# Expert weight rows to partitions in runs of eight (down: four), one contiguous 16 KB piece per partition

## The chip, the cores and the metric

The kernel runs on one core of a Trainium2 chip. The metric is the device time of one execution in microseconds (us); smaller is better. Three runs of the kernel before took 1603.82, 1595.23 and 1598.3 us, so the median is 1598.3 us.

## The reference

A two-layer backbone over 256 latent tokens and 256 context tokens of width 1024. Each layer has an attention mixer and then a mixture of experts. Cut to the part that matters here:

```python
def moe_ffn(h, w_router, b_router, w_gate, w_up, w_down):
    s = sigmoid(h @ w_router)                     # (N, 16)
    # one group of four experts, then the best two experts inside it
    out = 0
    for e in range(16):
        y = (silu(h @ w_gate[e]) * (h @ w_up[e])) @ w_down[e]   # 1024 -> 512 -> 1024
        out = out + combine[:, e:e + 1] * y
    return out
```

Layer 0 sends all 512 tokens through it, layer 1 only the 256 latent tokens. All weights are float32. The sum over the 1024 features (and over the 512 hidden units) may be taken in any order, as long as both operands of a product use the same one.

## The kernel before, in words

**Stages.** Twelve chunks of the modulation matrix (L529, each 2 MB), a norm and projections of layer 0, attention, the output projection with the second norm (`out_project`), the router and the lists of tokens per expert, then the experts; the same again for layer 1. TensorE, VectorE, ScalarE, GpSimd and SyncE each have their own program, tied together by semaphores that are written out by hand.

**Weights.** SyncE issues every weight load in program order into a ring of six slots of 16 KB per partition (`load`, L363 to L368). A load waits until the chunk that lay in its slot six chunks ago is used up (`chunks_used`). One expert takes three slots, gate, up and down, of 2 MB each, so the ring holds two experts.

**Layout of a chunk.** TensorE contracts over the 128 partitions, so the 1024 rows of gate and up are split in eight blocks of 128. Before, block k holds rows 128k to 128k+127 and partition p has row 128k+p of it: `"e (k p) f -> e p k f"` (L409, L410). In DRAM a partition's data are eight pieces of 2 KB that lie 256 KB apart. For down the 512 rows are four blocks of 128, four pieces of 4 KB per partition (L411).

**One expert** (`pair`, L754 on TensorE, L1281 on VectorE, L1666 on ScalarE). GpSimd gathers the expert's token rows from `h_dram` (L1857). TensorE transposes them in eight blocks (`rows_T`, L749); ScalarE writes the upper part (L1646), VectorE the rest (L1268). Weights are split likewise into an upper part (ScalarE, L1662) and a rest (VectorE, L1277), and 48 matmuls form gate and up (L767 to L769, three for each block and matrix). ScalarE applies silu (L1672), VectorE multiplies by up out of PSUM (L1287), TensorE transposes the product in four blocks (L779), ScalarE copies it (L1676), and 16 float32 matmuls with down follow (L788). The result goes to DRAM from ScalarE's queue (L1690). TensorE's order in one expert is written by hand: the 48 matmuls, the transposes of the next expert's rows, the four transposes of the product, the 16 matmuls of down.

**Before the experts** (`out_project`). For each tile of 128 tokens VectorE adds the attention result to x (L1182, L1187), ScalarE sums the squares (L1626), and VectorE writes the normed and modulated row into `htok` with two operations on 128x1024 (L1171, L1172). From there it is stored to `h_dram` (L1623) and transposed for the router (L677, L685). Layer 0 has four such tiles, layer 1 has two.

**At the start** SyncE issues three modulation chunks, six small broadcast loads (L393), the router's weights (L394), x and ctx (L395, L396) and then the other chunks. All seven small loads count on one semaphore, `wide_loaded`, on which VectorE waits before L1008. Behind L1008 on VectorE stand L1009, L1010 and the copy L1029, which TensorE needs before L520.

Of the kernel before, what the change touches and what calls it, by code (L numbers as in the profile page):

```python
# [22 lines left out]
P = 128  # L23
D = 1024
KD = D // P
SEQ, CTX = 256, 256
NT = (SEQ + CTX) // P
LT = SEQ // P
# [5 lines left out]
SLOTS = 6  # L34
# [78 lines left out]
def build(nc, a, consts_dram, out_dram, dbg=None, cap=P):  # L113
# [5 lines left out]
    ds = bass.ds  # L119
# [58 lines left out]
    with ctx:  # L178
# [56 lines left out]
        def mod(l, s, r):  # L235
# [48 lines left out]
        xg_hi, xg_lo = ([rq_r[:, (2 * j + i) * D:(2 * j + i + 1) * D].rearrange("p (k n) -> p k n", k=KD) for i in range(2)]  # L284
                        for j in range(2))

        def blocks_of(region, o, n):
            return region[:, o:o + n * CH].rearrange("p (k n) -> p k n", k=n)
        quarter = [[blocks_of(rz_r, 2 * D, 4)], [blocks_of(rz_r, 4 * D, 4)],
# [72 lines left out]
        def _(sp):  # L362
# [28 lines left out]
            modulation(M0, 0, 0, 3)  # L391
            for dst, src in wide:
                sp.dma_start(dst, src.partition_broadcast(P)).then_inc(sem("wide_loaded"), 16)  # L393
            sp.dma_start(wr_sb.rearrange("p (k e) -> p k e", k=KD), a["w_router"].rearrange("(k p) e -> p k e", p=P)).then_inc(sem("wide_loaded"), 16)  # L394
            sp.dma_start(xt[:, 0:LT, :], a["x"].rearrange("a (t p) d -> p (a t) d", p=P)).then_inc(sem("x_loaded"), 16)  # L395
            sp.dma_start(xt[:, LT:NT, :], a["ctx"].rearrange("a (t p) d -> p (a t) d", p=P)).then_inc(sem("x_loaded"), 16)  # L396
            modulation(M0 + 3, 0, 3, MODC - 3)
# [8 lines left out]
                load(n, slotk[n % SLOTS], view(a["even_w_out"][0], CH, i * CH))  # L406

            def experts(base, l):
                gate = a["w_gate"][l].rearrange("e (k p) f -> e p k f", p=P)  # L409
                up = a["w_up"][l].rearrange("e (k p) f -> e p k f", p=P)  # L410
                down = a["w_down"][l].rearrange("e (j p) d -> e p j d", p=P)  # L411
                with sp.Fori(0, NE // 2) as it:
                    for u in range(2):
                        e = it * 2 + u
                        for j, w in enumerate((gate, up, down)):
                            n = base + 3 * u + j
                            s = slotk[n % SLOTS] if j < 2 else slot[n % SLOTS].rearrange("p (j n) -> p j n", j=4)
                            load(n, s, w[ds(e, 1)].rearrange("e p k f -> (e p) k f"), it=it)

            def overflow(l):  # L420

                sp.wait_ge(sem(f"flag_set{l}"), at(f"flag_set{l}", 1))
                over = sp.value_load(flag_i[l][0:1, :], min_val=0, max_val=1)
                with sp.If(over > 0):
                    mats = [(a["w_gate"][l], FF), (a["w_up"][l], FF), (a["w_down"][l], D)]

                    sp.wait_ge(sem(f"y_v{l}"), at(f"y_v{l}", NE))
                    with sp.Fori(0, ROUNDS[l]) as r:
                        with sp.Fori(0, NE) as e:
                            for j in range(3):  # L430

                                if j == 0:
                                    sp.wait_ge(sem(f"over_xT{l}"), at(f"over_xT{l}", r * NE + e + 1))
                                else:
                                    sp.wait_ge(sem(f"over_used{l}"), at(f"over_used{l}", (r * NE + e) * 3 + j))
                                sp.dma_start(over_w[j], mats[j][0][ds(e, 1)].rearrange(
                                    "a (k p) n -> p (a k) n", p=P)).then_inc(sem(f"over_loaded{l}"), 16)
                sp.nop()
            modulation(MA, 1, *PARTS[0])
            experts(X0, 0)  # L440
# [530 lines left out]
        def _(ve):  # L971
# [188 lines left out]
            def out_project(l):  # L1160

                g = 0
                T = TL[l]

                def token_rows(t):
                    rms(rstd[:, t:t + 1], 1, t)
                    if t >= 2:

                        ve.wait_ge(sem(f"h_hi{l}"), at(f"h_hi{l}", t - 1))
                        ve.wait_ge(sem(f"h_stored{l}_{t % 2}"), at(f"h_stored{l}_{t % 2}", 16 * (t // 2)))  # L1170
                    link(V.scalar_tensor_tensor(htok[t % 2], xt[:, t, :], rstd[:, t:t + 1], bc[2 + t // LT], ALU.mult, ALU.mult))  # L1171
                    V.tensor_tensor(htok[t % 2], htok[t % 2], bc[4 + t // LT], ALU.add).then_inc(sem(f"h_ready{l}"), 1)  # L1172

                def token_cols(t):
                    ve.wait_ge(sem(f"h_lo{l}"), at(f"h_lo{l}", t + 1))
                    V.tensor_copy(hT[:, 0:4, t * P:(t + 1) * P], bank[4 + 2 * (t % 2)][:, :].rearrange("p (k n) -> p k n", k=4))\
                     .then_inc(sem(f"h_v{l}"), 1)
                for i in range(2):
                    for t in range(T):
                        product_done(ve, f"out_mm{l}", O0 if l == 0 else O1, [T, T], i, t)  # L1180
                        tm = rk[:, (g % 4) * 512:(g % 4 + 1) * 512]
                        ins = V.tensor_tensor(tm, bank[g % 4][:, :], bc[t // LT][:, i * 512:(i + 1) * 512], ALU.mult)  # L1182
                        ins.then_inc(sem(f"out_v{l}"), 1)
                        g += 1
                        ve.wait_ge(sem(f"out_v{l}"), at(f"out_v{l}", g))
                        xs = xt[:, t, i * 512:(i + 1) * 512]
                        V.tensor_tensor(xs, xs, tm, ALU.add).then_inc(sem(f"x_add{l}"), 1)  # L1187
                        if i == 0:
                            r = len(gate_list(l)) + t
                            broadcast(f"bc{l}", bc_list(l), range(r, r + 1))  # L1190
                        if i == 1:
                            if t >= 1:
                                token_cols(t - 1)
                            token_rows(t)
                token_cols(T - 1)

            def experts(l):
# [83 lines left out]
                def pair(it, last_pair):  # L1281
                    for u in range(2):
                        e = it * 2 + u
                        quarter_lo(u, e, 3)
                        ve.wait_ge(sem(f"silu_ready{l}"), at(f"silu_ready{l}", e + 1))
                        ve.wait_ge(chunks_used, e * 3 + (X0 if l == 0 else X1) + 2)
                        V.tensor_tensor(act_[u], sg[u], bank[3][:, :], ALU.mult).then_inc(sem(f"act_ready{l}"), 1)  # L1287
                        if not (last_pair and u == 1):
                            rows_lo(1 - u, e + 1)
                            for q in range(3):  # L1290
                                quarter_lo(1 - u, e + 1, q)
                        ve.wait_ge(sem(f"y_mm{l}"), at(f"y_mm{l}", e + 1))
                        ve.wait_ge(sem(f"y_stored{l}_{u}"), at(f"y_stored{l}_{u}", it * 16))
                        V.tensor_copy(ybuf[u][:, 0:512], bank[5][:, :]).then_inc(sem(f"y_v{l}"), 1)
# [12 lines left out]
                with ve.If(over > 0):  # L1307
                    ve.wait_ge(sem(f"y_stored{l}_0"), at(f"y_stored{l}_0", 8 * NE))
                    with ve.Fori(0, ROUNDS[l] * NE) as i:
# [2 lines left out]
                            V.tensor_copy(xgT[0][:, 4 * h:4 * h + 4, :], bank[h][:, :].rearrange("p (k n) -> p k n", k=4))\  # L1312
                             .then_inc(sem(f"over_xgT{l}"), 1)
                        ve.wait_ge(sem(f"over_silu{l}"), at(f"over_silu{l}", i + 1))
                        V.tensor_tensor(act_[0], sg[0], bank[3][:, :], ALU.mult).then_inc(sem(f"over_act{l}"), 1)
                        ve.wait_ge(sem(f"over_used{l}"), at(f"over_used{l}", i * 3 + 3))
                        for h in range(2):
                            V.tensor_copy(ybuf[0][:, 512 * h:512 * h + 512], bank[5 + h][:, :]).then_inc(sem(f"over_y{l}"), 1)
# [625 lines left out]
```

## Time and profile before

| | |
|---|---|
| median of three runs | 1598.3 us (1595.23 to 1603.82) |
| span of the profiled execution | 1598.7 us |
| TensorE busy | 1408.6 us, 88% of the span |
| VectorE, ScalarE busy | 803.2 us, 572.6 us |
| bytes moved | 327.33 MB, mean 205 GB/s |
| mean granted TensorE clock | 0.936 of full speed |

The span runs from the first to the last instruction of one profiled execution. It is the profiled execution's own time here and lies 0.4 us above the median of the runs. A matmul's row shows its duration, while matmuls follow one another more closely than that; the distance between starts is what an engine really spends. Idle time of an engine that nothing waits for costs nothing.

### The profile page before, as it was taken

The page shows a single profiled execution, that of the slowest core. Times are in us where ns is not written, and L with a number is a line of the kernel's source. Part 1 is how long each engine was busy: PE and PEld are TensorE (multiplying, and loading weights), DVE is VectorE, ACT ScalarE, POOL GpSimd, SP SyncE. Part 2 cuts the span into 40 slices and gives each one's busy share as a digit, 9 for nine tenths or more (in the row PEclk, how much of TensorE's full clock was granted, in tenths as well). Part 3 has the DMA queues.
Part 4 walks back from the last instruction along what each step waited for, and adds up shares of the span by engine and source line. Part 5 has one row for each costly group of instructions (what it writes and reads, how often), then busy time and mean ns, then how long its engine had stood idle before and what let it go on. Part 6 is the DMA issues. An engine that isn't in the chain of part 4 may idle for free.

```text
span 1598.7 us, 16348 instructions
## 1 busy us (share of the span) xinstructions
PE 1408.6 (88%) x6170; PEld 939.9 (59%) x6170; DVE 803.2 (50%) x1040; ACT 572.6 (36%) x830; POOL 115.7 (7%) x106
## 2 busy tenths in 40 slices
PE   6999959898977997999999999887994999999991
PEld 1229844477865544666666652756953666666660
DVE  0115231567865343555555536565835455555553
ACT  2004121235452113555555521513412444444451
POOL 0000032000000003000000004020002000000002
PEclk9999988898978998999999999897996999999996
DMA  9970000100007155999999999360012799999942
GB/s 328 385 249 35 0 0 27 53 1 1 1 1 263 66 190 177 349 363 363 362 361 363 350 335 347 115 237 18 1 53 98 259 364 362 363 363 362 362 172 92
DMA packets 138594, 327.33 MB, mean 205 GB/s; under 512 B 6133, under 2 KB 10538, under 8 KB 138410
## 3 DMA queue, kind: packets, MB, share of 16 engines
q1 hardware_dynamic: 125706, 282.43, 49.5%
q0 software_dynamic: 6784, 23.09, 3.9%
q10 hardware_dynamic: 6048, 21.04, 3.3%
q8 instruction: 37, 0.61, 0.2%
q14 instruction: 19, 0.16, 0.0%
HBM read 305.51 MB, written 21.04 MB: 204 GB/s over the span
## 4 chain that ended last, share of the span: by engine, by line
PE 78%; DVE 8%; ACT 6%; issue 3%; DMA 2%; POOL 1%; SPq 1%; POOLq 0%; DVEq 0%; ACTq 0%
PE bank L788 14%; PE bank L767 7%; PE bank L769 7%; PE bank L768 7%; PE bank L638 5%; PE bank L700 5%; PE bank L529 5%; PE bank L546 3%; PE bank L630 3%; PE bank L620 3%; PE bank L601 3%; PE bank L602 3%; PE bank L603 3%; ACT region_q_r L1646 2%; PE bank L861 1%
## 5 line engine op out<-in xcount | busy, mean ns | idle before, releaser
L1277 DVE TENSOR_TENSOR ring_r<-ring,region_z_r 128x2048 fp32r<-128x2048 f32 (+1 forms) x128 | 253.5, 2022 | 144.8 <-ACT region_z_r L1662 144.8
L788 PE MATMUL bank<-ring,region_h 128*128 128x512 f32 x512 | 228.2, 598 | 23.8 <-ACT region_h L1676 23.8
L1662 ACT ACTIVATE region_z_r<-ring 128x2048 fp32r<-128x2048 f32 (+1 forms) x128 | 210.0, 1691 | 75.7 <-PE bank L769 75.7
L768 PE MATMUL bank<-ring_r,region_q_r 128*128 128x512 f32 x512 | 200.6, 392 | 0.0
L767 PE MATMUL bank<-region_z_r,region_q_r 128*128 128x512 f32 x448 | 188.8, 421 | 2.8 <-DVE region_q_r L1268 2.8
L769 PE MATMUL bank<-region_z_r,region_q_r 128*128 128x512 f32 x448 | 176.0, 393 | 0.0
L788 PEld LDWEIGHTS bank<-ring,region_h 128*128 128x128 f32 x512 | 94.6, 190 | 138.4 <-issue 131.0
L638 PEld LDWEIGHTS bank<-region_z,region_h 128*128 128x128 f32 x832 | 113.9, 198 | 14.9 <-issue 7.1
L1601 ACT ACTIVATE region_h<-bank,small 128x512 f32<-128x512 f32 (+1 forms) x128 | 77.7, 607 | 123.6 <-DVE small L1125 103.6
L638 PE MATMUL bank<-region_z,region_h 128*128 128x64 f32 x832 | 111.0, 273 | 2.5 <-DVE region_h L1133 2.4
L768 PEld LDWEIGHTS bank<-ring_r,region_q_r 128*128 128x128 f32 x512 | 97.2, 190 | 26.6 <-issue 7.2
L767 PEld LDWEIGHTS bank<-region_z_r,region_q_r 128*128 128x128 f32 x448 | 85.1, 190 | 27.5 <-issue 6.7
L1133 DVE COPY region_h<-bank 128x512 f32<-128x512 f32 (+1 forms) x128 | 75.6, 591 | 41.9 <-PE bank L630 40.9
L1646 ACT ACTIVATE region_q_r<-bank 128x512 fp32r<-128x512 f32 x64 | 35.0, 595 | 170.7 <-PE bank L749 170.7
L769 PEld LDWEIGHTS bank<-region_z_r,region_q_r 128*128 128x128 f32 x448 | 84.9, 190 | 18.4
L529 PE MATMUL bank<-ring,small 128*2 128x512 f32 x192 | 90.2, 627 | 5.2 <-DMA ring<-in_w_mod 4.3
L601 PE MATMUL bank<-region_k_r,region_q_r 128*128 128x512 f32 (+3 forms) x256 | 88.8, 347 | 0.6 <-DVE ring_r L1055 0.6
L602 PE MATMUL bank<-ring_r,region_q_r 128*128 128x512 f32 (+3 forms) x256 | 88.3, 345 | 0.0
L603 PE MATMUL bank<-region_k_r,region_h_r 128*128 128x512 f32 (+3 forms) x256 | 88.3, 345 | 0.0
L1287 DVE TENSOR_TENSOR region_h<-region_h,bank 128x512 f32<-128x512 f32 x32 | 22.0, 688 | 126.0 <-PE bank L769 126.0
L546 PE MATMUL bank<-ring,small 128*2 128x512 f32 x192 | 84.3, 592 | 0.8 <-issue 0.5
L700 PE MATMUL bank<-ring,region_q 128*128 128x512 f32 x192 | 84.1, 593 | 0.0
(257 smaller groups left out, 1847.2 us busy)
## 6 DMA issues: line engine op xcount, KB each, us to landing
ring<-in_w_gate SPq DMA_DIRECT2D x32, 2048.0 KB, 9.5
ring<-in_w_up SPq DMA_DIRECT2D x32, 2048.0 KB, 11.0
ring<-in_w_down SPq DMA_DIRECT2D x32, 2048.0 KB, 9.7
ring<-in_w_mod SPq DMA_DIRECT2D x24, 2048.0 KB, 17.2
y_rows<-region_k ACTq DMA_DIRECT2D x32, 512.0 KB, 7.7
ring<-in_even_w_in SPq DMA_DIRECT2D x3, 2048.0 KB, 7.8
ring<-in_even_w_out SPq DMA_DIRECT2D x2, 2048.0 KB, 8.0
ring<-in_odd_w_in SPq DMA_DIRECT2D x2, 2048.0 KB, 13.2
```

Of the source, the lines that this page charges most:

```text
L529: last = mm(bank[j % 2][0:2, :], silu.rearrange("p (r k) -> p k r", r=2)[:, k, :], slotk[(M0 + j) % SLOTS][:, k, :], start=k == 0, stop=k ...
L601: mm(out, hh, wh, start=k == 0, stop=False)
L602: mm(out, hh, wl, start=False, stop=False)
L603: last = mm(out, hl, wh, start=False, stop=k == KD - 1)
L638: last = mm(out, probsT[(b + u - 1) % 2][:, j * P:(j + 1) * P], v, start=j == 0, stop=j == len(vs) - 1)
L700: last = mm(bank[g % 4][:, :], oT[:, k, t * P:(t + 1) * P], slotk[n % SLOTS][:, k, :], start=k == 0, stop=k == KD - 1)
L767: mm(bank[2 + j][:, :], xg_hi[u][:, k, :], wh, start=k == 0, stop=False)
L768: mm(bank[2 + j][:, :], xg_hi[u][:, k, :], wl, start=False, stop=False)
L769: last = mm(bank[2 + j][:, :], xg_lo[u][:, k, :], wh, start=False, stop=k == KD - 1)
L788: last = mm(bank[5 + h][:, :], actT[u][:, j, :], w[:, j, h * 512:(h + 1) * 512], start=j == 0, stop=j == 3)
L1277: ins = V.tensor_tensor(slotk_r[s_][:, k:k + n, :], slotk[s_][:, k:k + n, :], part.bitcast(f32), ALU.subtract)
L1662: ins = A(part, slotk[n % SLOTS][:, k:k + m, :], ACT.Copy)
```

## The change

Partition p now holds rows 8p to 8p+7 of gate and up and rows 4p to 4p+3 of down, which is one contiguous piece of 16 KB in DRAM. Block k of the contraction is then made of the rows 8p+k. The other operand follows: `htok` is written so that its k-th block of 128 columns holds the features 8j+k, by reading x and the two modulation rows with a step of eight elements; the router's weights are loaded in the same order; and the product of silu and up is written so that block k holds the hidden units 4j+k, by reading both inputs with a step of four elements. The writes stay contiguous. Number, order and shape of instructions on each engine stay as they are.

```diff
+        def strided(ap, n):
+            return ap.rearrange("p (j k) -> p k j", k=n)
...
-            sp.dma_start(wr_sb.rearrange("p (k e) -> p k e", k=KD), a["w_router"].rearrange("(k p) e -> p k e", p=P)).then_inc(sem("wide_loaded"), 16)
+            sp.dma_start(wr_sb.rearrange("p (k e) -> p k e", k=KD), a["w_router"].rearrange("(p k) e -> p k e", p=P)).then_inc(sem("wide_loaded"), 16)
...
-                gate = a["w_gate"][l].rearrange("e (k p) f -> e p k f", p=P)
-                up = a["w_up"][l].rearrange("e (k p) f -> e p k f", p=P)
-                down = a["w_down"][l].rearrange("e (j p) d -> e p j d", p=P)
+                gate = a["w_gate"][l].rearrange("e (p k) f -> e p (k f)", p=P)
+                up = a["w_up"][l].rearrange("e (p k) f -> e p (k f)", p=P)
+                down = a["w_down"][l].rearrange("e (p j) d -> e p (j d)", p=P)
...
-                            s = slotk[n % SLOTS] if j < 2 else slot[n % SLOTS].rearrange("p (j n) -> p j n", j=4)
-                            load(n, s, w[ds(e, 1)].rearrange("e p k f -> (e p) k f"), it=it)
+                            load(n, slot[n % SLOTS], w[ds(e, 1)].rearrange("e p f -> (e p) f"), it=it)
...
-                    link(V.scalar_tensor_tensor(htok[t % 2], xt[:, t, :], rstd[:, t:t + 1], bc[2 + t // LT], ALU.mult, ALU.mult))
-                    V.tensor_tensor(htok[t % 2], htok[t % 2], bc[4 + t // LT], ALU.add).then_inc(sem(f"h_ready{l}"), 1)
+                    ht = htok[t % 2].rearrange("p (k j) -> p k j", k=KD)
+                    link(V.scalar_tensor_tensor(ht, strided(xt[:, t, :], KD), rstd[:, t:t + 1], strided(bc[2 + t // LT], KD), ALU.mult, ALU.mult))
+                    V.tensor_tensor(ht, ht, strided(bc[4 + t // LT], KD), ALU.add).then_inc(sem(f"h_ready{l}"), 1)
...
-                        V.tensor_tensor(act_[u], sg[u], bank[3][:, :], ALU.mult).then_inc(sem(f"act_ready{l}"), 1)
+                        V.tensor_tensor(act_[u].rearrange("p (k j) -> p k j", k=4), strided(sg[u], 4), strided(bank[3][:, :], 4), ALU.mult).then_inc(sem(f"act_ready{l}"), 1)
```

The loads and the product of the overflow branch (L436, L1315), which runs only when an expert gets more than 128 tokens, are changed in the same way.

## Rows read from the trace of the kernel before

**Rows 1.** The page: the span of the profiled execution
```profile
span 1598.7 us, 16348 instructions
```

**Rows 2.** A stretch of the experts: PE PEld DVE ACT POOL busy, clock, DMA share, GB/s
```profile
1430.00:1470.00 40.00, 38.48 (x152) 26.26 (x151) 23.27 (x18) 19.95 (x21) 1.89 (x2) 1.00 0.99 363
```

**Rows 3.** Who waited for whom, 680 to 940 us: PE's wait (us, times, longest)
```profile
PE bank L788 <- ACT region_h L1676: 9.8, 13, 0.8
```

**Rows 4.** Instructions in order of time, one expert of layer 1: start, us, engine, line
```profile
1297.81 7.13 PE L788 MATMUL bank<-ring,region_h 128*128 128x512 f32 x16 [0.76 <-ACT region_h L1676]
...
1310.62 0.37 SPq L368 DMA_DIRECT2D ring<-in_w_gate  x1
...
1315.48 1.02 PEld L749 LDWEIGHTS bank<-con,region_k 128*128 128x128 f32 x8
...
1315.90 0.69 DVE L1287 TENSOR_TENSOR region_h<-region_h,bank 128x512 f32<-128x512 f32 x1 [3.92 <-PE bank L769]
1316.34 1.08 ACT L1646 ACTIVATE region_q_r<-bank 128x512 fp32r<-128x512 f32 x2 [5.28 <-PE bank L749]
...
1316.65 0.66 PE L779 MATMUL bank<-con,region_h 128*128 128x128 f32 x4
1317.34 0.60 ACT L1676 ACTIVATE region_h<-bank 128x512 f32<-128x512 f32 x1
...
1318.07 7.13 PE L788 MATMUL bank<-ring,region_h 128*128 128x512 f32 x16 [0.76 <-ACT region_h L1676]
```

**Rows 5.** The page: two DMA queues (weights; stores); then issue of a load to landing
```profile
q1 hardware_dynamic: 125706, 282.43, 49.5%
...
q10 hardware_dynamic: 6048, 21.04, 3.3%
...
ring<-in_w_gate SPq DMA_DIRECT2D x32, 2048.0 KB, 9.5
```

**Rows 6.** Groups of VectorE by line and shape: busy us, mean ns of one
```profile
L1287 DVE TENSOR_TENSOR region_h<-region_h,bank 128x512 f32<-128x512 f32 x32 | 22.0, 688 | 126.0 <-PE bank L769 126.0
...
L1171 DVE SCALAR_TENSOR_TENSOR region_k<-x,small,region_z 128x1024 f32<-128x1024 f32 x6 | 7.7, 1285 | 0.2
L1172 DVE TENSOR_TENSOR region_k<-region_k,region_z 128x1024 f32<-128x1024 f32 x6 | 7.4, 1225 | 0.2
```

**Rows 7.** VectorE multiplies by a per-partition scalar, by line: min/median/max ns
```profile
L1406 DVE TENSOR_SCALAR small<-small x4: 234/235/235, 436.8 to 488.5; 128x8 f32<-128x8 f32 x4
...
L1343 DVE TENSOR_SCALAR region_z<-region_z,small x4: 341/1884/2431, 229.3 to 239.9; 128x256 f32<-128x256 f32 x4
...
L1049 DVE TENSOR_SCALAR region_z<-x,small x8: 752/754/2767, 119.0 to 1002.4; 128x1024 f32<-128x1024 f32 x8
```

**Rows 8.** Instructions in order of time, out_project: two rows of each layer
```profile
551.51 1.23 DVE L1172 TENSOR_TENSOR region_k<-region_k,region_z 128x1024 f32<-128x1024 f32 x1
...
553.60 1.04 PE L677 MATMUL bank<-con,region_k 128*128 128x128 f32 x8
...
1207.88 1.22 DVE L1172 TENSOR_TENSOR region_k<-region_k,region_z 128x1024 f32<-128x1024 f32 x1
...
1209.16 1.97 PE L677 MATMUL bank<-con,region_k 128*128 128x128 f32 x8
```

**Rows 9.** The start: chain; PE's gap; issue to landing of b_router, of L368's second load
```profile
17.35 12.19 DMA small<-in_w_router
...
43.23 6.96 PE bank L529 x16
...
31.19 1.86 PE L520 MATMUL bank<-con,region_k 2*128 2x2 f32 x8 [2.88 <-DVE region_k L1029]
...
small<-in_b_router SPq DMA_DIRECT2D x1, 8.0 KB, 9.1
...
L368 SPq DMA_DIRECT2D ring<-in_w_mod x2: 3604/3996/4389, 22.7 to 26.4; - x2
...
DMA to landing us min/median/max: 19.1/19.1/19.1
```

More of the change, by code:

```diff
@@ L436, in overflow @@
                                 sp.dma_start(over_w[j], mats[j][0][ds(e, 1)].rearrange(
-                                    "a (k p) n -> p (a k) n", p=P)).then_inc(sem(f"over_loaded{l}"), 16)
+                                    "a (p k) n -> p (a k) n", p=P)).then_inc(sem(f"over_loaded{l}"), 16)
                 sp.nop()
@@ L1314, in experts @@
                         ve.wait_ge(sem(f"over_silu{l}"), at(f"over_silu{l}", i + 1))
-                        V.tensor_tensor(act_[0], sg[0], bank[3][:, :], ALU.mult).then_inc(sem(f"over_act{l}"), 1)
+                        V.tensor_tensor(act_[0].rearrange("p (k j) -> p k j", k=4), strided(sg[0], 4), strided(bank[3][:, :], 4), ALU.mult).then_inc(sem(f"over_act{l}"), 1)
                         ve.wait_ge(sem(f"over_used{l}"), at(f"over_used{l}", i * 3 + 3))
```

## The prediction

> **What bounds the kernel now.** I began with the span, 1598.7 us [rows 1], 0.4 us above the median of the runs shown; every sum below is made against it. Next I took the busy time by stretch, because the change promises faster weight loads and these matter only where something waits for them. During the experts the DMA engines look full: a share of 0.99 at 363 GB/s, while TensorE is busy 38.48 of 40 us at a granted clock of 1.00 [rows 2]. Both could be the bound, so the list of waits decides. From 680 to 940 us, thirteen experts, TensorE waits for ScalarE's copy L1676 (13 times 0.75 us) and for no DMA [rows 3]. The timeline says the same. Two L788 groups start 1318.07 - 1297.81 = 20.26 us apart. The load of a gate chunk issued at 1310.62 lands 9.5 us later, at 1320.1, and its slot is first read while the next expert's down product runs, from 1318.07 + 20.26 = 1338.3 [rows 4, 5]. It is ready about 18 us early. So the experts are bound by TensorE and by the short chain that it waits for, and the DMA engines are busy because they are asked for just that much: 3 x 2 MB of weights plus two transfers of 0.5 MB, 7.34 MB in 20.26 us, are 362 GB/s.
>
> The chain is what the reader should see in rows 4. TensorE loads its last row transposes (L749) until 1316.50. The four transposes of the product (L779) start only at 1316.65, right after VectorE's product L1287 has ended at 1315.90 + 0.69 = 1316.59. They end at 1317.31, ScalarE's copy L1676 starts at 1317.34, and L788 after it. L1287 thus has no slack at all: each ns that it grows is a ns per expert.
>
> **The change part by part.**
>
> *Weight loads.* The same 96 loads of 2 MB, now 128 pieces of 16 KB each. Nothing waits for them, so their gain is costed at nothing; the cover is the 18 us above. Are large pieces slower? The weight queue moved 282.43 MB in 125706 packets with 49.5% of 16 engines' span: 0.495 x 16 x 1598.7 / 125706 = 101 ns for a mean of 2247 B, 22.3 B/ns. The queue of the stores has mean packets of 3479 B and 0.033 x 16 x 1598.7 / 6048 = 140 ns each, 24.9 B/ns [rows 5]. Larger packets go faster here. I expect a smaller DMA share and no time. SyncE issues as many DMAs at the same points as before; what a load issued earlier or landed earlier would trigger is nothing, since each issue waits for a used chunk.
>
> *Router weights.* A partition's 512 B come as one piece instead of eight of 64 B. This one is on the path: VectorE waits for the load until 17.35 + 12.19 = 29.54, and TensorE stands for 2.88 us until 31.19 [rows 9]. The small load just ahead of it in the queue, b_router, has 128 pieces and takes 9.1 us from issue to landing; the router's has 1024 and takes 12.19 [rows 9]. With 128 pieces it should land at 17.35 + 9.1 = 26.5, and the gap closes: a gain of 2.9 us. It can't be much more, for the fourth modulation chunk is late next. The fifth is issued at 26.4 and lands 19.1 us later, at 45.5; the fourth lies 2 MB ahead of it, 5.8 us at 363 GB/s, so it lands near 39.7, and TensorE now takes it at 43.23 [rows 2, 9]. Bounds 0 (the load stays slow) and 43.2 - 39.7 = 3.5 us.
>
> *Strided reads on VectorE, the main term.* L1287 reads both inputs with a step of 16 B (one of them in PSUM), L1171 and L1172 read with a step of 32 B; writes stay contiguous. No large operation of the trace does this, so the price is bounded. From below: nothing; L1287 takes 688 ns and L1172 1225 ns for twice the elements, 1.05 ns per element, and a read with a step may well keep that rate [rows 6]. From above I use the nearest row, L1406: eight elements, read and written in place with a step of 16 B (heads lie four floats apart), by a per-partition scalar. Its contiguous kin, L1343 with 256 elements at 341 ns at least and L1049 with 1024 at 752 ns, give 0.535 ns per element and a fixed 204 ns, so eight contiguous elements would take 208 ns. L1406 takes 235 [rows 7]. The 27 ns over are up to 3.4 ns per element, 3.9 in all; if I take the fixed part from L1049 alone, at half the 1.05 ns above (220 ns), it is 1.9 ns per element in all. The row is small and its excess may belong to the instruction and not to its elements. I take 2.1 ns, twice the contiguous rate, since L1406 is the nearest row by its step and this lies at the careful end of its 1.9 to 3.9. Then L1287 grows by 512 x 1.04 = 0.53 us and L1171 and L1172 by 1.07 us each.
>
> Where this lands:
> - L1287, 32 experts, no slack: 32 x 0.53 = +17.0 us (bounds 0 and 32 x 1.46 = 47). Behind it on VectorE stand the rests of the rows and weights; VectorE is busy 23.27 of 40 us [rows 2], so they have room.
> - Layer 1, two tiles: L1172 of the second tile ends at 1209.10 and TensorE's L677 follows at 1209.16 [rows 8]. VectorE is the path through both tiles, since L1182 of the second stands right behind L1172 of the first: 2 x 2 x 1.07 = +4.3 us.
> - Layer 0, four tiles: L1172 of the first ends at 552.74, TensorE comes for it at 553.60 behind other products [rows 8]. Of 2.13 us, 0.86 is covered: +1.3 us. The later tiles have more cover as TensorE's products of the output projection take 7 us each; I put +0.1 on them.
>
> Sum: 1598.7 + 17.0 + 4.3 + 1.4 - 2.9 = 1618.5 us, +1.2%.
>
> L1406 spends more than its contiguous kin [rows 7]. The Trainium skill has a rule that would make it so and that speaks against this change: "SBUF — State Buffer", section Door 1: The DMA port swizzle, tells of 16-byte lines that want at least two accesses each for full rate, which a step of four floats never gives. By that rule, with which rows 7 agree as far as they reach, the time lies above 1595.8 us; it names no price.
>
> **The rivals.**
>
> *R1, strided reads cost nothing.* VectorE takes one float32 element per cycle wherever it lies, and L1406's 27 ns are fixed cost. For it: rows 6 have 1.05 ns per element for PSUM and SBUF inputs alike. Against it: rows 7. Time: 1598.7 - 2.9 = 1595.8, no change by the measure. This is the other side of my forecast; it decides at a price of 0.13 ns per element: there the strided terms, 22.7 us at 1.04 ns, are 2.9 us and the start pays for them. The Trainium skill's page "VectorE: DVE Perf Modes", section Mode 1× (REGULAR) — the baseline, would give this time: it says that this mode works with any step, at one result per cycle.
>
> *R2, a steeper price,* near the 3.9 ns bound, say because the PSUM input is worse than SBUF. L1287 +1.46 us, 47 us; L1171 and L1172 +2.9 us each, about 12 us in layer 1 and 7 in layer 0: 1598.7 + 66 - 3 = 1662. Only the upper reading of one small row speaks for it. A price of 3.1 ns, twice my increase, would give about 1642.
>
> *R3, the 16 KB pieces are slow.* Few long pieces per engine could lower the rate. The ring hides it until a layer's 15 further periods have eaten 18 us, so 1.2 us per period, a rate under 7.34 MB / 21.5 us = 342 GB/s. At 300 GB/s a period is 24.5 us and the time 1598.7 + 2 x (15 x 4.2 - 18) = 1689. Rows 5 speak against it.
>
> *R4, the loads are cut into small pieces again,* so the change is not what it says. Then the packets stay as many, and no term of my sum moves, for the loads were costed at nothing.
>
> **How the numbers follow.** A measurement of this kernel tells about 0.5% (8 us) from no change. Twice the rate cost, or near it (1610 to 1626): 0.50. R1: 0.37, times from 1593 to 1599. R2: 0.06. R3: 0.03. A gain over 8 us, from the start and from landings that I do not see: 0.04. R4 changes none. Slower 0.58, same 0.37, faster 0.05 follow (a small price between R1 and mine lies on the border). The range has to take in R1, so 1592 to 1625; the forecast's own range is 1610 to 1626.
>
> **What would show it.** Right: L1287 at about 1.22 us, L1171 and L1172 at about 2.3 us; the distance of L788 groups 20.8 instead of 20.26 us with TensorE idle about 0.7 us before L779; the router's load landing near 26.5 us and L520 starting at about 28.4; the weight queue with some 70000 packets fewer (the experts' 64 x 1024 + 32 x 512 become 96 x 128) and a DMA share below 0.99. Wrong: L1287 still at 0.69 us (R1), far above 1.3 us (R2), a wait of ScalarE's L1662 or TensorE's L788 for a DMA (R3), or 125706 packets again (R4).

## The result, and the profile after

The changed kernel took 1617.9 us (median of four runs, 1614.9 to 1619.8) beside 1598.1 us (1595.2 to 1603.8) for the kernel before: a ratio of 1.0108, 95% interval 1.0081 to 1.0135, so 12.9 to 21.6 us longer. The profiled execution has a span of 1616.0 us. In its lines L1287 has become L1291, L1171 and L1172 have become L1175 and L1176, L749 L752, L779 L782, L788 L791, L677 L680, L520 L523, L529 L532, L546 L549, L1029 L1032; the issues of x (L395) and of the chunks (L368) are L399 and L372.

The page, span and weight queue (packets, MB, share of 16 engines):

```profile
span 1616.0 us, 16348 instructions
...
q1 hardware_dynamic: 55178, 282.43, 47.0%
```

The groups of VectorE by line and shape (busy us, mean ns), the answer to [rows 6]:

```profile
L1291 DVE TENSOR_TENSOR region_h<-region_h,bank 128x512 f32<-128x512 f32 x32 | 34.7, 1083 | 125.9 <-PE bank L772 125.9
...
L1175 DVE SCALAR_TENSOR_TENSOR region_k<-x,small,region_z 128x1024 f32<-128x1024 f32 x6 | 12.5, 2091 | 0.2
L1176 DVE TENSOR_TENSOR region_k<-region_k,region_z 128x1024 f32<-128x1024 f32 x6 | 12.1, 2018 | 0.2
```

The product went from 688 to 1083 ns, 0.395 us or 0.77 ns per element more; the two operations on `htok` grew by 806 and 793 ns for 1024 elements, 0.79 and 0.77 ns per element. A step of 16 B and one of 32 B cost the same for each element.

One expert of layer 1 in order of time (start, us, engine, line, and in brackets how long the engine stood before it and for whom), the answer to [rows 4]:

```profile
1310.37 7.13 PE L791 MATMUL bank<-ring,region_h 128*128 128x512 f32 x16 [0.76 <-ACT region_h L1680]
...
1328.46 1.09 DVE L1291 TENSOR_TENSOR region_h<-region_h,bank 128x512 f32<-128x512 f32 x1 [3.92 <-PE bank L772]
1328.90 1.09 ACT L1650 ACTIVATE region_q_r<-bank 128x512 fp32r<-128x512 f32 x2 [5.28 <-PE bank L752]
1329.61 0.66 PE L782 MATMUL bank<-con,region_h 128*128 128x128 f32 x4 [0.31 <-DVE region_h L1291]
1330.30 0.60 ACT L1680 ACTIVATE region_h<-bank 128x512 f32<-128x512 f32 x1 [0.31 <-PE bank L782]
1331.02 7.13 PE L791 MATMUL bank<-ring,region_h 128*128 128x512 f32 x16 [0.76 <-ACT region_h L1680]
```

The distance of two down groups is 20.65 us here and 20.64 us on average, against 20.24 before: 0.39 us, as much as the product has grown. TensorE now stands 0.31 us in front of L782, a wait that [rows 4] don't have; the 0.76 us in front of L791 is the old one. The stretch that answers to [rows 2] shows the same from the other side: TensorE busy 37.87 of 40 us instead of 38.48, while the DMA engines have fallen from 0.99 to 0.91 and nobody gains by it.

```profile
1430.00:1470.00 40.00, 37.87 (x149) 25.57 (x148) 24.03 (x18) 20.58 (x20) 1.89 (x2) 1.00 0.91 352
```

`out_project` of the changed kernel in order of time: the first tile of layer 0, then both of layer 1 [rows 8]:

```profile
548.53 1.09 PE L680 MATMUL bank<-con,region_k 128*128 128x128 f32 x8 [0.64 <-DVE region_k L1176]
...
1212.72 1.10 PE L680 MATMUL bank<-con,region_k 128*128 128x128 f32 x8 [1.87 <-DVE region_k L1176]
...
1219.95 1.97 PE L680 MATMUL bank<-con,region_k 128*128 128x128 f32 x8 [0.58 <-DVE region_k L1176]
```

The chain of waits at the start of the changed kernel, the answer to [rows 9]:

```profile
17.71 10.15 DMA small<-in_w_router
...
30.55 6.96 PE bank L532 x16
...
38.49 6.97 PE bank L532 x16
```

The router's load now takes 10.15 instead of 12.19 us. What else the start shows has to wait for a second profile of the kernel before, below.

### The profile page after: what moved, and what is told of

It reads as the page before. It is cut to its first block, busy times and chain, and to the rows that moved or that the text cites. A ratio compares the mean times of both kernels' runs of the same rounds, so it can differ in the third digit from the quotient of the medians.

```text
span 1616.0 us, 16348 instructions
## 1 busy us (share of the span) xinstructions
PE 1413.7 (87%) x6170; PEld 942.9 (58%) x6170; DVE 824.7 (51%) x1040; ACT 574.5 (36%) x830; POOL 113.4 (7%) x106
## 4 chain that ended last, share of the span: by engine, by line
PE 78%; DVE 10%; ACT 4%; issue 3%; DMA 2%; POOL 1%; SPq 1%; POOLq 0%; DVEq 0%; ACTq 0%
PE bank L791 14%; PE bank L770 7%; PE bank L772 7%; PE bank L771 7%; PE bank L641 5%; PE bank L532 4%; PE bank L703 4%; PE bank L549 4%; PE bank L633 3%; PE bank L623 3%; PE bank L604 3%; PE bank L606 3%; PE bank L605 3%; DVE region_h L1291 2%; PE bank L864 1%
## 5 line engine op out<-in xcount | busy, mean ns | idle before, releaser
L791 PE MATMUL bank<-ring,region_h 128*128 128x512 f32 x512 | 229.8, 602 | 23.8 <-ACT region_h L1680 23.8
L791 PEld LDWEIGHTS bank<-ring,region_h 128*128 128x128 f32 x512 | 95.3, 191 | 139.4 <-issue 132.0
L771 PEld LDWEIGHTS bank<-ring_r,region_q_r 128*128 128x128 f32 x512 | 97.2, 190 | 26.5 <-issue 7.2
L1291 DVE TENSOR_TENSOR region_h<-region_h,bank 128x512 f32<-128x512 f32 x32 | 34.7, 1083 | 125.9 <-PE bank L772 125.9
L532 PE MATMUL bank<-ring,small 128*2 128x512 f32 x192 | 85.4, 600 | 5.7 <-DMA ring<-in_w_mod 4.7
L549 PE MATMUL bank<-ring,small 128*2 128x512 f32 x192 | 87.7, 612 | 0.8 <-issue 0.5
```

What stands on the lines that cost most here:

```text
L532: last = mm(bank[j % 2][0:2, :], silu.rearrange("p (r k) -> p k r", r=2)[:, k, :], slotk[(M0 + j) % SLOTS][:, k, :], start=k == 0, stop=k ...
L549: last = mm(bank[2 + j % 2][0:2, :], silu.rearrange("p (r k) -> p k r", r=2)[:, k, :], slotk[(base + j) % SLOTS][:, k, :], start=k == 0, s ...
L771: mm(bank[2 + j][:, :], xg_hi[u][:, k, :], wl, start=False, stop=False)
L791: last = mm(bank[5 + h][:, :], actT[u][:, j, :], w[:, j, h * 512:(h + 1) * 512], start=j == 0, stop=j == 3)
```

## The experiments

The theories to be told apart: the time comes from VectorE's stepped accesses (my forecast); from the long pieces, which hold up other transfers; or from something in the new order that neither names. Later, which operand and which step pays, and whether the start and the token list's path moved because of the change at all.

### Down in its old order: the product contiguous again

```diff
-                down = a["w_down"][l].rearrange("e (p j) d -> e p (j d)", p=P)
+                down = a["w_down"][l].rearrange("e (j p) d -> e p j d", p=P)
...
-    V.tensor_tensor(act_[u].rearrange(...), strided(sg[u], 4), strided(bank[3][:, :], 4), ALU.mult)
+    V.tensor_tensor(act_[u], sg[u], bank[3][:, :], ALU.mult)
```

> The changed kernel with down loaded in its old order (four pieces of 4 KB per partition) and silu times up multiplied without a step. Theory (reads with a step cost 0.40 us of TensorE's path per expert): the product takes 0.69 us again, an expert 20.25 us, and the time falls by 32 x 0.40 = 12.7 us against the changed kernel, to about 1605 us. Rival (the 16 KB pieces cost the time): two thirds of the bytes still come in 16 KB pieces, so two thirds of the loss stay, 1612 us or more.

It took 1604.4 us beside 1602.1 for the kernel before, ratio 1.0015 (1.0004 to 1.0025). The product is back at 687 ns and the distance of down groups at 20.24 us, while L1178 and L1179, the operations on `htok` here, still take 2090 and 2025 ns. So one stepped instruction per expert is worth 1.0108 - 1.0015 = 0.93% or 14.9 us of the difference; by the two intervals it may be 10 to 20 us, and 32 x 0.395 = 12.6 us lies in that.

### The long pieces alone

The kernel before with the loads of gate, up and down changed; router, `htok` and product are left as they were. The features then meet rows of weights that aren't theirs; the amount of work is the same.

```diff
-                gate = a["w_gate"][l].rearrange("e (k p) f -> e p k f", p=P)
+                gate = a["w_gate"][l].rearrange("e (p k) f -> e p (k f)", p=P)
```

> The kernel before, with only the expert weights loaded in one 16 KB piece per partition; router, features and activations keep the old order, so the experts multiply features with rows of weights that don't belong to them. Theory: nothing waits for these loads, so the time is that of before within 3 us; an expert takes 20.25 us; the first gather of layer 0, which runs beside a weight load, lands up to 2 us later; the DMA share in the experts falls from 0.99 to about 0.93. Rival (the pieces cost): 1610 us or more and a wait for a DMA in the experts.

It took 1604.3 us beside 1602.1, ratio 1.0011 (0.9995 to 1.0026), with a distance of 20.25 us in both layers and a DMA share of 0.92. TensorE waits for no weight load. Fewer, longer pieces neither cost nor gain anything that the time shows; a cost of up to 4 us lies within the interval.

### The router's load on its own semaphore, in the kernel before

```diff
-  a["w_router"].rearrange("(k p) e -> p k e", p=P)).then_inc(sem("wide_loaded"), 16)
+  a["w_router"].rearrange("(k p) e -> p k e", p=P)).then_inc(sem("router_loaded"), 16)
...
-        SMALL_LOADS, WIDE_LOADS = 8, 7
+        SMALL_LOADS, WIDE_LOADS = 8, 6
```

TensorE waits for `router_loaded` only before its first product with the router's weights.

> The kernel before, with the router's load counted on a semaphore of its own: VectorE's first operations wait for the six broadcasts alone, TensorE waits for the router's load ahead of the output projection. Theory (the start gained because VectorE no longer waits long for the router's load): TensorE's gap at 28 to 31 us goes, the fourth modulation chunk starts some 5 us earlier, and the time is 5 to 6 us less than before. Rival (the start gained from fewer pieces in the queue, which bring the modulation chunks in sooner): the gap goes, but the fourth chunk's load is late instead, and the gain is 3 us or less.

It took 1601.1 us beside 1601.6, ratio 0.9998 (0.9985 to 1.0011). The 5 to 6 us of the first theory are refuted, and the rival came true: TensorE's gap shrinks to 0.66 us, but then the fourth chunk is late. The chain at its start shows it:

```profile
23.25 16.98 DMA ring<-in_w_mod
40.27 10.00 PE bank L529 x16
```

With VectorE released, TensorE runs into the fourth modulation chunk, which lands at 40.2. That is the cap which the prediction put at 39.7: in the kernel before, the wait for the router mostly stands in front of a wait that would come anyway. The chunk's matmuls then take 10.00 us in this profile, at a clock that fell after the wait, and 7.03 in the second profile of the kernel before. This profile is of the slowest of the ten executions (1605.4 us), so the 10.00 may not be typical.

### The same permutation by stepped writes

The operations read contiguously and write with the step, `act_[u].rearrange("p (k j) -> p j k", k=4)` and the like for `htok`.

> The changed kernel with the same permutation made by writes with a step (512 B) and contiguous reads, in the two operations on the token rows and in silu times up. Theory (only a read with a step of 16 B or more is slow, for its two accesses a line): the product takes 0.69 us, the token rows 1.29 and 1.23 us (one of the three reads htok with the step in the second operation, which may cost), and the time is about 1602 us. Rival (any step in an operand costs the same): 1.08 and 2.1 us as in the changed kernel, and its time, 1618 us.

Along the innermost dimension the writes now have a step of 128 elements (512 B). It took 1618.3 us beside 1602.1, ratio 1.0100 (1.0074 to 1.0126). Its groups:

```profile
L1292 DVE TENSOR_TENSOR region_h<-region_h,bank 128x512 f32<-128x512 f32 x32 | 33.7, 1052 | 125.9 <-PE bank L772 125.9
...
L1176 DVE SCALAR_TENSOR_TENSOR region_k<-x,small,region_z 128x1024 f32<-128x1024 f32 x6 | 12.0, 2000 | 0.2
L1177 DVE TENSOR_TENSOR region_k<-region_k,region_z 128x1024 f32<-128x1024 f32 x6 | 11.5, 1921 | 0.2
```

A write with a step of 512 B costs 0.71 ns per element, nearly what stepped reads cost, so the theory that only reads pay is refuted. Moving the step to the other side of the product saves 0.03 us. A write with a step of 16 B was not run.

### TensorE takes the step instead

VectorE is contiguous everywhere; the transposes read every eighth column of `htok` and of the gathered rows, and every fourth of the product.

```diff
-  ins = tr(..., htok[t % 2][:, k * P:(k + 1) * P], ident)
+  ins = tr(..., strided(htok[t % 2], KD)[:, k, :], ident)
...
-  last = tr(..., act_[u][:, j * P:(j + 1) * P], ident)
+  last = tr(..., strided(act_[u], 4)[:, j, :], ident)
```

> The changed kernel with all VectorE operands contiguous again; instead the transposes on TensorE read the token rows with a step of 32 B and the product with a step of 16 B, so every result is the same. Theory A (a step of 16 B slows whatever engine reads it): a transpose's load takes about 1.8 times as long, 12 of them per expert at some 64 to 127 ns, so an expert takes 20.25 us plus 0.5 to 1.2 us and the time is 1610 us or more. Theory B (the price is VectorE's own, 1.8 ns per element instead of 1.04): an expert takes 20.25 us and the time is that of before less the start's 5 to 6 us, about 1593 us, which would beat both kernels.

It took 1601.9 us beside 1601.6, ratio 0.9999 (0.9987 to 1.0012), distance of down groups 20.34 us. That is neither the 1610 us of theory A nor the 1593 of theory B. Its groups of weight loads:

```profile
L752 PEld LDWEIGHTS bank<-con,region_k 128*128 128x128 f32 x256 | 34.2, 190 | 27.5 <-issue 25.0
...
L782 PEld LDWEIGHTS bank<-con,region_h 128*128 128x128 f32 x128 | 17.9, 209 | 5.8 <-DVE region_h L1290 3.5
```

In the changed kernel these lines have 145 and 141 ns. TensorE's loads pay as well, but they lie beside matmuls, and what is left is 0.10 us of the 0.39 us per expert.

### Which step and which operand

Three kernels differ from the changed one in L1291 alone, and mix hidden units for it: a step of two elements (8 B) on both inputs; a step of four on silu, in SBUF, alone; a step of four on up, in PSUM, alone.

> The changed kernel with silu times up read with a step of two elements (8 B) in place of four; hidden units and rows of down don't match then. By 16-byte lines that want two accesses each, a step of 8 B still makes two per line in SBUF: the product takes 0.69 us. If PSUM's lines are 8 B, or if any step costs, it takes 1.08 us or something between.

> The changed kernel with only silu's result (SBUF) read with a step of 16 B in the product; the factor in PSUM is read contiguously, so the product mixes hidden units. If each stepped operand slows the operation by itself, 1.08 us as with both; if it was PSUM alone, 0.69 us; if the two prices add, about 0.89 us.

> The changed kernel, in which VectorE's product of silu and up reads only up, its input in PSUM, with a step of four elements (16 B); silu is read contiguously. (The product then pairs different hidden units; the amount of work is the same.) The sibling run with only silu stepped took 1.083 us for the product, as much as both stepped. Theory A: the step costs the engine, whichever operand has it: the product again takes 1.06 to 1.10 us, the distance of two down products stays at 20.62 to 20.66 us, the time is near 1615 to 1618. Theory B: only SBUF pays for a 16 B step and PSUM doesn't: the product takes 0.69 us, the distance is 20.24 us, the time near 1603. A third value between the two would mean that the two memories have prices of their own.

The group of the product in each, in this order:

```profile
L1291 DVE TENSOR_TENSOR region_h<-region_h,bank 128x512 f32<-128x512 f32 x32 | 22.0, 688 | 126.3 <-PE bank L772 126.3
```

```profile
L1291 DVE TENSOR_TENSOR region_h<-region_h,bank 128x512 f32<-128x512 f32 x32 | 34.7, 1083 | 125.9 <-PE bank L772 125.9
```

```profile
L1291 DVE TENSOR_TENSOR region_h<-region_h,bank 128x512 f32<-128x512 f32 x32 | 22.0, 687 | 126.2 <-PE bank L772 126.2
```

The times, of one execution each, agree: 1603.1, 1615.2 and 1604.8 us, with distances of 20.24, 20.64 and 20.24 us. The whole price of the changed kernel's product comes from its SBUF input. The PSUM input, which R2 suspected, may be stepped for nothing, and so may an SBUF input by 8 B. A step of 12 B was not run, so where between 8 and 16 B the price begins isn't shown.

### The kernel before, profiled once more

> The kernel before once more, for a second profile of it. What is to be seen is how much the stages before layer 0's experts differ from one profile to the next. Theory A: the dips of TensorE's granted clock in the modulation stage are a matter of how the first chunks land, so the end of that stage lies within 1 us of the first profile, and the path from the first scatter of the token list to the landing of the first gather takes 25.0 us within 1 us. Theory B: the stage ends and the list's path move by 2 us or more between two profiles of one kernel; then what I read as the small pieces' and the large pieces' effect there (4 us sooner, 2.6 us later) is no more than the spread.

It took 1599.1 us, span 1597.2. The modulation stage's matmuls (line, count, min/median/max ns, first and last start) in the first profile of the kernel before, in this one, and in the changed kernel:

```profile
L529 PE MATMUL bank<-ring,small x192: 592/592/1061, 11.9 to 115.3; 128*2 128x512 f32 x192
```

```profile
L529 PE MATMUL bank<-ring,small x192: 589/592/1061, 11.7 to 110.6; 128*2 128x512 f32 x192
```

```profile
L532 PE MATMUL bank<-ring,small x192: 589/592/1061, 12.2 to 109.2; 128*2 128x512 f32 x192
```

Between two profiles of one kernel the stage ends 4.7 us apart. The stretch from 30 to 40 us says what differs, again the first profile and then the second:

```profile
30.00:40.00 10.00, 8.81 (x20) 3.00 (x21) 1.66 (x5) 5.42 (x11) 0.00 (x0) 0.66 1.04 390
```

```profile
30.00:40.00 10.00, 9.18 (x33) 3.29 (x34) 2.12 (x4) 5.55 (x11) 0.00 (x0) 1.00 1.05 393
```

The granted clock is 0.66 in one and 1.00 in the other, that is part of the stretch at 1.2 instead of 2.4 GHz, and 20 matmuls fall into it instead of 33. Before the fall TensorE had stood for the router's load in both. From 60 to 80 us the first profile has another such stretch (0.91) and the second doesn't. So theory B of this run holds: of the 6.1 us by which the changed kernel ends this stage sooner than [rows 9]'s profile, 4.7 are this clock, and 110.6 - 109.2 = 1.4 us may be the change. TensorE's start on the fourth chunk says the same: 39.79 in the second profile, 38.43 in the changed kernel. I had read all of it as a gain of the router's load, until this profile.

The list's path, from the first scatter L1846 to the first transpose of gathered rows in layer 0, took 25.1 us in the first profile, 27.3 in this and 27.4 in the run with the router's own semaphore, all with short pieces; with long ones it took 26.7 in the changed kernel and 28.4 to 29.9 in seven others. The long pieces may cost 2 us here, but the two groups overlap and one execution apiece doesn't settle it.

### Hold the weights back while the list is written, in the kernel before

```diff
                         s = slotk[n % SLOTS] if j < 2 else ...
+                        if (l, u, j) == (0, 1, 1):
+                            sp.wait_ge(sem("xg_loaded0_0"), at("xg_loaded0_0", 16))
```

> The kernel before plus one wait on SyncE: in layer 0 it issues expert 1's up load and all after it only when the first expert's token rows have landed. Six chunks otherwise fill the DMA engines just when the token list is scattered, read back and used for the first gather, a path of 25.0 us in the profile of before. Theory A (the small transfers queue behind the weights): with fewer loads under way the path shortens to about 20 us and the time falls by 3 to 5 us, to a ratio of 0.997 to 0.998, and no later wait for weights shows, as the ring is 18 us ahead. Theory B: the path is made of fixed costs of each transfer and of the other engines, it stays at 25 us and the time doesn't change. Theory C: the loads held back are late for experts 1 to 3, TensorE waits for a DMA there, and the time rises by up to 10 us.

It took 1597.2 us beside 1601.7, ratio 0.9970 (0.9954 to 0.9986): 4.8 us. GpSimd's rows from the last scatter on, in the second profile of the kernel before and then in this one (in brackets what GpSimd waited for the scatters and for the list):

```profile
610.59 0.59 POOL L1849 DMA_DIRECT2D small_i<-slot_list  x1 [6.33 <-DMA slot_list<-small_i]
616.87 1.16 POOL L1857 DMA_INDIRECT region_k<-h_rows,small_i  x1 [5.70 <-DMA small_i<-slot_list]
```

```profile
608.69 0.59 POOL L1851 DMA_DIRECT2D small_i<-slot_list  x1 [1.63 <-DMA slot_list<-small_i]
610.90 1.00 POOL L1859 DMA_INDIRECT region_k<-h_rows,small_i  x1 [1.62 <-DMA small_i<-slot_list]
```

With no new 2 MB loads started beside them both waits are about a quarter as long as in the second profile. Against other executions the gain is less sure: they were 5.45 and 2.45 us in the first profile, 5.95 and 1.54 in the changed kernel. So the wait for the scatters is shorter than in all of these, and the wait for the list varies by itself. The path is 18.4 us long, 7 to 9 us less than in the two profiles. Most of this is lost again in a new wait, the longest of TensorE between 590 and 700 us:

```profile
PE bank L769 <- DVE region_q_r L1270: 7.0, 1, 7.0
```

L1270, VectorE's rest of the rows, now stands behind four L1279 (the rests of the weights, 6.76 us in the chain) that VectorE does first in the hand-written order. The kernel before waits 1.4 us at this place. The first product with gate starts 26.5 us after the first scatter, against 28.5 and 30.6 us in the two profiles: 2 to 4 us of gain, which agrees with the 4.8 us of the runs within their interval (2.2 to 7.4). Doing L1270 first is the next thing to try; it wasn't tried.

### The layout without its price

Two kernels combine this. The first keeps down in its old order, so that the product is contiguous, lets TensorE's transposes of the token rows take the step of eight, and holds the loads back:

```diff
-   htok[t % 2][:, k * P:(k + 1) * P]   ...   xg[buf][:, k * P:(k + 1) * P]
+   strided(htok[t % 2], KD)[:, k, :]   ...   strided(xg[buf], KD)[:, k, :]
```

> The changed kernel made free of VectorE's stepped reads: down keeps its old order and so the product is contiguous (0.69 us); the normed rows are written contiguously (1.28 and 1.23 us) and TensorE's transposes of them and of the gathered rows take every eighth column (a step of 32 B) instead; gate, up and the router stay in 16 KB or 512 B pieces; and SyncE holds back expert 1's up load in layer 0 as in the run beside this one. Theory A: TensorE's stepped weight loads lie beside its matmuls, for the distance of down products stays at 20.25 to 20.30 us; the start brings 3 to 6 us, the held-back loads 3 to 5 us, and the time is 1589 to 1594, a ratio of 0.994 to 0.996. Theory B: the stepped weight loads (190 ns instead of 145 in the run with all transposes stepped) cost about 0.1 us per expert, 3 us in all, and the held-back loads bring nothing: 1598 to 1601, no gain. Theory C: the gain at the start is given back on the list's path as in the runs before.

It took 1594.2 us beside 1601.7, ratio 0.9956 (0.9939 to 0.9972), distance 20.24 us.

The second keeps the changed kernel's whole layout, down too, and uses that PSUM reads are free: ScalarE's silu reads its bank with the step and writes contiguously.

```diff
-   A(sg[u], bank[2][:, :], ACT.Silu)
+   A(sg[u].rearrange("p (k j) -> p k j", k=4), strided(bank[2][:, :], 4), ACT.Silu)
...
-   V.tensor_tensor(..., strided(sg[u], 4), strided(bank[3][:, :], 4), ALU.mult)
+   V.tensor_tensor(..., sg[u].rearrange("p (k j) -> p k j", k=4), strided(bank[3][:, :], 4), ALU.mult)
```

> The whole layout of the changed kernel, gate, up and down in 16 KB pieces, with every step of 16 B or more moved off the SBUF operands of VectorE: ScalarE's silu now reads its PSUM bank with a step of four elements and writes contiguously, VectorE's product reads that contiguously and up out of PSUM with a step of four, TensorE's transposes take every eighth feature as in the run that held the loads back, and the loads are held back in the same place. Theory A (only SBUF operands pay for such a step, on ScalarE too): silu stays at 0.60 us and the product at 0.69 us, the distance of two down products is 20.24 us, and the time is that of the kernel with down in its old order, 1591 to 1596, a ratio of 0.994 to 0.997 to the kernel before. Theory B: ScalarE pays for a step in PSUM although VectorE doesn't: silu takes about 1.0 us, it stands on the path to the product, which then ends 0.4 us later, and the distance becomes 20.6 us and the time 1603 to 1608. If the 16 KB pieces of down hurt anything, the time rises with silu and product unchanged.

It took 1594.6 us beside 1602.7, ratio 0.9961 (0.9945 to 0.9978). Product and silu:

```profile
L1292 DVE TENSOR_TENSOR region_h<-region_h,bank 128x512 f32<-128x512 f32 x32 | 22.0, 688 | 126.2 <-PE bank L774 126.2
...
L1677 ACT ACTIVATE region_h<-bank 128x512 f32<-128x512 f32 x32 | 19.2, 600 | 24.5 <-PE bank L774 24.5
```

Silu has its 600 ns of the changed kernel and the distance is 20.25 us. Theory A held in the second run. In the first its ratio and distance held and the time lies at its upper end; the 3 to 6 us that it expected from the start aren't shown. Both beat both kernels, but most of that is the held-back loads, which alone give 0.9970; the intervals of the three overlap, so a further gain of the layout (2.2 and 1.4 us by the ratios) isn't shown.

## Why the prediction was right, step by step

The forecast was 1618.5 us and the median 1617.9, for the mechanism that it named. Its terms came out like this:

| term | forecast | measured |
|---|---|---|
| product, 32 experts | +17.0 | 32 x 0.39 = +12.5 |
| layer 1, two tiles | +4.3 | +3.2 |
| layer 0, four tiles | +1.4 | +0.8, and +1.3 by the clock |
| router's load | -2.9 | about -1.4 |
| weight loads | 0 | 0 |
| sum | +19.8 | +16.4 |

By the measured ratio the change costs 1.0108 x 1598.7 - 1598.7 = +17.3 us (12.9 to 21.6). That the total came so close is in part luck: the product was taken 4.5 us too large, and much of that came back by a gain of the router that was 1.5 us too large and a clock that I had not foreseen. The profiled span is 1616.0 - 1597.2 = 18.8 us over the second profile of the kernel before; beside the 16.4 it holds 1.6 us of one down group at the lower clock (the kernel with stepped writes has 8.83 us at this place, all others 7.13), 1.3 us more in layer 1 between this group and `out_project`, with no new wait, and 0.6 us less on the list's path (26.7 against 27.3). That is 18.7 of the 18.8. The down group:

```profile
950.37 8.75 PE L791 MATMUL bank<-ring,region_h 128*128 128x512 f32 x16 [0.69 <-ACT region_h L1680]
```

*The price.* The step that was mis-sized is "I take 2.1 ns, twice the contiguous rate". It is 0.77 ns on top of 1.05, 1.82 in all. That this is near the 1.9 which I had read as the lower of L1406's two readings is luck: with half of 1.05 ns, as the text says, the fixed part is 752 - 1024 x 0.525 = 214 ns and the reading (235 - 214) / 8 = 2.6; the 1.9 comes from 0.52. At 0.77 ns each, eight elements explain 6 of the 27 ns by which L1406 exceeds its kin [rows 7]; what the other 21 are isn't shown. A row with eight elements could not carry a price per element. R1, the other side with 0.37, is refuted for this step and would hold for a step of 8 B. R2 is refuted: the PSUM input adds nothing. The Trainium skill, "SBUF — State Buffer", section Door 1: The DMA port swizzle, gave the rule that a 16-byte line of SBUF wants at least two accesses. The runs agree with it on both sides: at 8 B, two floats of each line, the product takes 688 ns, and at 16 B, one float, 1083. What that section concludes from its rule, that one can stride over four fp32 for free, is refuted by these runs if it means a step of four. The same section gives PSUM lines of 8 bytes and a penalty for matmuls; VectorE's and ScalarE's stepped PSUM reads (687 and 600 ns) show none.

*Without slack.* "Each ns that it grows is a ns per expert" is right: 0.395 us of product, 0.39 us of distance. I had expected 0.7 us of idle time before L779, and it is 0.31. A row of the kernel before, from the stretch of [rows 4], has the rest:

```profile
1315.70 1.03 PE L749 MATMUL bank<-con,region_k 128*128 128x128 f32 x8
```

These matmuls end at 1316.73 and overlap L779 (from 1316.65) by 0.08 us; 0.31 + 0.08 is the 0.39.

*The tiles.* In layer 1 the first tile's transposes slip by 1.5 us against the output projection ahead of them and the second's by 1.7 us more. In layer 0 the first tile slips by 0.8 us, about the two increments of 0.8 less the cover of 0.86 that [rows 8] gave. What I put at 0.1 for the later tiles came out as 1.3, and not through VectorE: eight matmuls of the second modulation stage run at a lower clock. The kernel before, then the changed one:

```profile
589.10 3.60 PE L546 MATMUL bank<-ring,small 128*2 128x512 f32 x8 [0.31 <-ACT region_z L1634]
```

```profile
584.08 5.29 PE L549 MATMUL bank<-ring,small 128*2 128x512 f32 x8 [0.31 <-ACT region_z L1638]
```

*The router.* "With 128 pieces it should land at 26.5" took the time of b_router (9.1 us) for a load that has as many pieces but eight times the bytes. It landed after 10.15 us, at 27.86, and the gap did not close. It is 2.03 us, against 2.88 and 3.02 us in the two profiles of the kernel before:

```profile
29.50 1.05 PE L523 MATMUL bank<-con,region_k 2*128 2x2 f32 x8 [2.03 <-DVE region_k L1032]
```

The end of the gap comes 1.3 us sooner than in the second profile (30.82), and this can reach the next stage only because the cap, the late fourth chunk, moved too. I had written that SyncE issues its loads at the same points as before. It does not, as its issues behind the router's load show, in the kernel before and then in the changed one:

```profile
18.03 4.01 SPq L395 DMA_DIRECT2D x<-in_x  x1
...
22.74 40.78 SPq L368 DMA_DIRECT2D ring<-in_w_mod  x8
```

```profile
18.39 0.64 SPq L399 DMA_DIRECT2D x<-in_x  x1
...
19.75 41.79 SPq L372 DMA_DIRECT2D ring<-in_w_mod  x8
```

The issue of x takes 0.64 us behind a router's load of 128 pieces and 4.01 behind one of 1024 (4.02 in the kernel that has only the long expert pieces), so the fourth chunk is issued 3.0 us sooner and TensorE doesn't wait for it. Of the 2.9 us forecast, 1.4 are left.

*The loads.* 70528 packets fewer, as the forecast had it, a DMA share down by 0.08, and no wait for weights anywhere, so R3 and R4 fell at once. That nothing was gained is the cover of 18 us that the ring has.

## What to carry to other kernels

A layout that pleases the DMA engines is paid for by whoever has to follow it. Before the step goes to an elementwise instruction, look whether that instruction has slack, and whether the step can go where it is free: into a PSUM operand, down to 8 B in SBUF, or, nearly free, into weight loads that lie beside matmuls. And a full-looking queue (0.99 here) is worth a gain only if someone waits for it; here the one who waited was a list of 8 KB, scattered and read back beside the weights. Holding those back gave a gain that the runs show (0.9970), and no run shows one of the new layout.

## What was not expected of the hardware

- The price depends on where the stepped operand lies and not on how many there are. For 512 float32 elements on VectorE: 688 ns contiguous, 688 with 8 B on both inputs, 687 with 16 B in PSUM, 1083 with 16 B in SBUF, whether the PSUM input is stepped too or not, 1052 with a write of 512 B step. L1175 has two stepped inputs in SBUF and L1176 one, and they grew by 0.79 and 0.77 ns per element.
- TensorE's weight loads of transposes take 141 ns contiguous and 209 with a step of 16 B (L782), 145 and 190 with one of 32 B (L752).
- The clock after the stepped tiles. In all six kernels with stepped operations on `htok` the eight matmuls above take 5.29 us, in all eight profiles without them 3.60. In the changed kernel the sixteen after them are slow too, 8.72 instead of 7.03 us, in front of a wait for the gathered rows that hides it. From 585 to 590 us the granted clock of the changed kernel is 0.66, and 1.00 in the kernel before. TensorE had been busy 19.36 of the 20 us from 545 to 565 in the changed kernel, where it waited for the first tile, and 20.00 in the kernel before. Why the clock falls there stays open.
- Two profiles of one kernel, with spans 1.5 us apart, differ by 4.7 us in a stage. A difference between two kernels in a stage that is bound by neither's change needs a second profile of the first.
